# A hybrid two-layer decoder trunk: state-space pairs turned back by VectorE instead of GpSimd, gate channel computed in column groups, mixer order and start cut differently

## The reference, cut to what matters

```python
h = x + 0.5 * swiglu(rms(x))                 # 1024 -> 2 x 2816 -> 1024
u = rms(h);  proj = u @ w_in                 # one projection feeds four mixers
y_sb  = stick_breaking_attention(q, k, v)    # 4 heads of 64
y_s5  = s5_mixer(s5_u, ...)                  # 16 groups, 1024 complex states
y_gla = gla_mixer(gq, gk, gv, gr, gg, ...)   # z = gg @ w_gate, gg is 16 channels wide
y_dsa = dilated_mixer(q, k, v, ...)
per_branch = einsum('bsnw,nwd->bsnd', branches, w_branch)
mixed = sum(sigmoid(gates) * per_branch)     # gates: 4 x 1024 channels of proj
h = h + mixed @ w_out
h = h + 0.5 * swiglu(rms(h))
```

## Time and profile before

| | |
|---|---|
| median of three runs | 1290.23 us |
| profiled execution | 1289.22 us, span 1287.3 us |
| PE busy | 1245.8 us (97%) |
| DVE / ACT / POOL busy | 895.5 / 640.0 / 327.4 us |
| weight rounding: ACT L812, DVE L1072 | 407.2 us, 518.0 us |
| mixer of layer 0 | about 222 to 440 us of the span |
| mixer of layer 1 | about 858 to 1076 us |
| granted PE clock, mean | 0.992 |

### The profile page before, as it was taken

How to read it: one execution, slowest core, us unless ns; L and a number is a source line. 1 busy time by engine, 2 the same in 40 slices (tenths; PEclk the granted TensorE clock), 3 DMA queues, 4 the chain that set the end, 5 groups by cost and what they waited for, 6 DMA issues and landing times.

```text
span 1287.3 us, 25597 instructions
## 1 busy us (share of the span) xinstructions
PE 1245.8 (97%) x10328; PEld 1222.4 (95%) x10328; DVE 895.5 (70%) x1172; ACT 640.0 (50%) x904; POOL 327.4 (25%) x462
## 2 busy tenths in 40 slices
PE   5999999999999999999999999999999999999998
PEld 5999999888999999999999999998889999999998
DVE  4766857877877676555676687687887786656554
ACT  5654545663544454444456445557625444534432
POOL 0388800364003300000005895005630041000000
PEclk9999999998999999999999999999999999999999
DMA  7555554542344365555545545544333454555541
GB/s 299 199 185 174 180 179 165 175 149 99 131 158 166 135 236 198 191 195 168 191 135 201 188 165 200 189 164 152 135 130 131 154 186 160 201 184 175 186 173 66
DMA packets 31029, 220.46 MB, mean 171 GB/s; under 512 B 3568, under 2 KB 3568, under 8 KB 4592
## 3 DMA queue, kind: packets, MB, share of 16 engines
q1 hardware_dynamic: 30960, 219.49, 49.0%
HBM read 218.42 MB, written 1.05 MB: 170 GB/s over the span
## 4 chain that ended last, share of the span: by engine, by line
PE 75%; DVE 12%; POOL 7%; ACT 3%; issue 2%; DMA 0%; DVEq 0%; SPq 0%; ACTq 0%
PE banks L456 24%; PE banks L457 24%; PE banks L458 24%; DVE w_lo_t L1072 5%; PE banks L469 3%; ACT w_hi_t L812 1%; POOL st L1631 1%; DVE s5x L1274 1%; POOL s5x L1629 1%; POOL s5x L1628 1%; POOL st L1634 1%; POOL st L1536 1%; POOL st L1632 1%; DVE u_lo_t L1084 1%; DVE hT L1223 1%
## 5 line engine op out<-in xcount | busy, mean ns | idle before, releaser
L1072 DVE TENSOR_TENSOR w_lo_t<-raw,w_hi_t 128x1024 fp32r<-128x1024 f32 x408 | 518.0, 1310 | 107.8 <-ACT w_hi_t L812 107.4
L812 ACT ACTIVATE w_hi_t<-raw 128x1024 fp32r<-128x1024 f32 x408 | 407.2, 1046 | 126.7 <-PE banks L458 126.0
L456 PE MATMUL banks<-u_hi_t,w_hi_t 128*128 128x256 f32 x1520 | 436.0, 287 | 18.2 <-DVE w_lo_t L1072 14.1
L457 PE MATMUL banks<-u_lo_t,w_hi_t 128*128 128x256 f32 x1520 | 431.9, 284 | 0.0
L458 PE MATMUL banks<-u_hi_t,w_lo_t 128*128 128x256 f32 x1520 | 431.9, 284 | 0.0
L456 PEld LDWEIGHTS banks<-u_hi_t,w_hi_t 128*128 128x128 f32 x1520 | 293.6, 193 | 22.5 <-DVE w_lo_t L1072 14.1
L457 PEld LDWEIGHTS banks<-u_lo_t,w_hi_t 128*128 128x128 f32 x1520 | 293.8, 193 | 0.1
L458 PEld LDWEIGHTS banks<-u_hi_t,w_lo_t 128*128 128x128 f32 x1520 | 293.5, 193 | 0.0
L456 PE MATMUL banks<-b_hi_t,w_hi_t 128*128 128x256 f32 x864 | 245.1, 284 | 1.9 <-DVE b_lo_t L1084 1.9
L457 PE MATMUL banks<-b_lo_t,w_hi_t 128*128 128x256 f32 x864 | 244.5, 283 | 0.0
L458 PE MATMUL banks<-b_hi_t,w_lo_t 128*128 128x256 f32 x864 | 244.5, 283 | 0.0
(11 more groups left out here) (215 smaller groups left out, 1267.7 us busy)
## 6 DMA issues: line engine op xcount, KB each, us to landing
raw<-weights SPq DMA_DIRECT2D x203, 1024.0 KB, 4.9
prm<-params SPq DMA_DIRECT2D x1, 1178.5 KB, 5.3
prm<-params SPq DMA_DIRECT2D x1, 1166.5 KB, 15.1
cst<-constants SPq DMA_DIRECT2D x1, 1027.0 KB, 11.1
hT<-x_t SPq DMA_DIRECT2D x2, 512.0 KB, 5.5
raw<-weights SPq DMA_DIRECT2D x2, 512.0 KB, 6.4
out_t<-hT SPq DMA_DIRECT2D x4, 256.0 KB, 2.2
prm<-params SPq DMA_DIRECT2D x1, 12.0 KB, 1.9
```

The lines of the kernel that those rows point to most:

```text
L456: pe.matmul(o, st[0], mv[0], start=start, stop=False, skip_group_check=True)
L457: pe.matmul(o, st[0], mv[1], start=False, stop=False, skip_group_check=True)
L812: act.activation(w_hi[:, slot, a:a + HALF], raw[:, slot, a:a + HALF], ACT.Copy) \
L1072: dve.tensor_tensor(w_lo[:, slot, a:a + HALF], raw[:, slot, a:a + HALF], w_hi[:, slot, a:a + HALF].bitcast(F32), ALU.subtract).then_inc(s. ...
```

## The change

- `s5_pair` leaves POOL. DVE gets `s5_back`: two products of 128x1024 and two sums of 128x512 for each pair, and `s5_rotate`, `s5_scan`, `s5_back` of a pair now stand together in DVE's `pieces(m)`, m = 1, 4, 7, 10. PE's `s5_out` stands two blocks after `s5_in` instead of four.
- Block "gg" is gone. PE's `gate_channels` in `pieces(1)` computes the 16 channels from u_hi and u_lo with 16 fp32 matmuls (K 128, 32 output columns) that go round four column groups of the array; a `w_gate` with its rows repeated four times sums the groups.
- `SEQ` has 30 entries: without gg, with (0,1) before gv, and with (1,2), (1,3) before (0,2), (0,3). `OUT_TILES` has six: tiles 4 and 5 get a block each.
- DVE at index 22 and at `out3`, and ACT at `out3`, do their steps in another order; PE's `out0` waits for three of the four b_lo, and for the fourth just before it is used.
- At the start x and the first weight block come in quarters, and PE's first block waits for each quarter by itself. ACT gets one tiny activation before x lands.
- Constants shrink by 127 columns, parameters grow by 144.

```diff
-SEQ = ["s5u", "sbq", "sbk", "gg", "gqk", "dq", "dk", (0, 0), "sbv", "gv", (0, 1), "dv", "gr", (1, 0), (1, 1),
-       (0, 2), (0, 3), (1, 2), (1, 3), (2, 0), (2, 1), (2, 2), (2, 3),
+SEQ = ["s5u", "sbq", "sbk", "gqk", "dq", "dk", (0, 0), "sbv", (0, 1), "gv", "dv", "gr", (1, 0), (1, 1),
+       (1, 2), (1, 3), (0, 2), (0, 3), (2, 0), (2, 1), (2, 2), (2, 3),
        (3, 0), "out0", (3, 1), "out1", (3, 2), "out2", (3, 3), "out3"]
-OUT_TILES = [(0, 1), (2, 3), (4, 5), (6,), (7,)]
+OUT_TILES = [(0, 1), (2, 3), (4,), (5,), (6,), (7,)]
-MIXED_AT = [((0,), (1,)), ((), ()), ((), ()), ((2, 3, 4, 5, 6), (7,))]
+MIXED_AT = [((0,), (1,)), ((), ()), ((), ()), ((2, 3, 4, 5), (6, 7))]
...
# PE
+                    def gate_channels():
+                        for n, (part, half) in enumerate(itertools.product(range(2), range(2))):
+                            for j in range(4):
+                                kt = 4 * half + j
+                                a = PARAM["w_gg"][0] + 16 * kt
+                                ins = single(banks[32 * j:32 * j + 32, 2, T:2 * T], prm[:, a:a + 32],
+                                             u_hi[:, kt, :].bitcast(F32) if part == 0 else u_lo[:, kt, :].bitcast(F32),
+                                             n == 0, n == 3)
+                        ins.then_inc(s.gg, 1)
                     def pieces(m):
+                        if m == 1:
+                            gate_channels()
                         if m in S5_AT:
                             s5_in(S5_AT.index(m))
-                        if m - 4 in S5_AT:
-                            s5_out(S5_AT.index(m - 4))
+                        if m - 2 in S5_AT:
+                            s5_out(S5_AT.index(m - 2))
...
                         if q == 0:
-                            pe.wait_ge(s.b_lo, layer * PER.b_lo + 4)
+                            pe.wait_ge(s.b_lo, layer * PER.b_lo + 3)
...
                             for n in range(4):
+                                if (q, dt, n) == (0, 0, 3):
+                                    pe.wait_ge(s.b_lo, layer * PER.b_lo + 4)
...
# ACT, start
+            act.activation(nrm[:, 0, :], prm[:, 0:2], ACT.Copy)
+            act.wait_ge(s.w_used, 1)
+            for q in range(4):
+                split_pair(0, "g_ffn1", q)
+                act.wait_ge(s_first[q] if q < 3 else landed[0], 16)
+                a = QUARTER * q
+                act.activation(w_hi[:, 0, a:a + QUARTER], raw[:, 0, a:a + QUARTER], ACT.Copy) \
+                    .then_inc(s.q_hi if q % 2 == 0 else s.w_hi, 1)
...
# DVE
+                def s5_back(pair):
+                    dve.wait_ge(s.s5_scan, layer * PER.s5_scan + pair + 1)
+                    if pair >= 1:
+                        dve.wait_ge(s.s5_y, layer * PER.s5_y + pair)
+                    wide = lambda x: x[:, 2 * pair:2 * pair + 2, :].unsqueeze(2).to_broadcast([P, 2, 2, T])
+                    dve.tensor_tensor(st[:, :, :, :], s5x[:, :, 1, :, :], wide(rotS), ALU.mult)
+                    own.link(dve.tensor_tensor(s5x[:, :, 0, :, :], s5x[:, :, 1, :, :], wide(rotC), ALU.mult))
+                    dve.tensor_tensor(st[:, :, 1, :], s5x[:, :, 0, 0, :], st[:, :, 1, :], ALU.subtract)
+                    dve.tensor_tensor(st[:, :, 0, :], s5x[:, :, 0, 1, :], st[:, :, 0, :], ALU.add) \
+                        .then_inc(s.s5_state, 1)
...
                     if m in S5_AT:
                         s5_rotate(S5_AT.index(m))
-                    if m - 1 in S5_AT:
-                        s5_scan(S5_AT.index(m - 1))
+                        s5_scan(S5_AT.index(m))
+                        s5_back(S5_AT.index(m))
...
                         if is_branch(m):
                             q = int(SEQ[m][3])
+                            gate(2 * q)
                             if q == 3:
                                 for dt in range(2, 6):
                                     mixed_lo(dt)
-                            gate(2 * q)
+                                gate(2 * q + 1)
                             rest_of_weights(layer, k0 + m // RING + 1, m % RING)
-                            gate(2 * q + 1)
+                            if q < 3:
+                                gate(2 * q + 1)
                             continue
...
+                        if m == 22:
+                            pieces(m)
                         rest_of_weights(layer, k0 + m // RING + 1, m % RING)
...
# POOL
-                for pair in range(ST // 2):
-                    s5_pair(pair)
```

More of the change, by code:

```diff
@@ L389, in build @@
         s.pool = sem("pool")
-        s_x = [sem("x_landed0"), sem("x_landed1")]
+        s_x = [sem(f"x_landed{q}") for q in range(4)]
         s_gain = sem("gains_landed")
-        s_first = sem("first_half_landed")
+        s_first = [sem(f"first_quarter_landed{q}") for q in range(3)]
         s_const = sem("const_landed")
@@ L473, in block_ready, with in_part, in_block @@
                     pe.wait_ge(s.w_lo, layer * PER.w_lo + 2 * b + 8)
-                def in_part(b, slot, bank, where, kts, tiles=2):
+                def in_part(b, slot, bank, where, kts):
                     for kt in kts:
-                        for ct in range(tiles):
-                            last = kt == KT - 1 and ct == tiles - 1
+                        for ct in range(2):
+                            last = kt == KT - 1 and ct == 1
                             three(banks[:, bank, ct * T:(ct + 1) * T], w(slot, kt * 256 + ct * P, P),
                                   act_tiles(kt, where=where), kt == 0 and ct == 0, last, s.w_used if last else None)
-                def in_block(b, slot, bank, where=0, tiles=2):
+                def in_block(b, slot, bank, where=0):
                     block_ready(b)
-                    in_part(b, slot, bank, where, range(KT), tiles)
+                    in_part(b, slot, bank, where, range(KT))
                 def first_two(b, bank, norm, where):
                     for n, (j, q) in enumerate(STRAIGHT):
-                        if q == 0:
+                        if layer == 0 and norm == 0 and j == 0:
+                            if q % 2 == 0:
+                                pe.wait_ge(s.q_lo, q // 2 + 1)
+                            else:
+                                pe.wait_ge(s.w_lo, 2 * RING + (q + 1) // 2)
+                        elif q == 0:
                             block_ready(b + j)
@@ L600, in s5_out @@
                     def s5_out(pair):
-                        pe.wait_ge(s.s5_state, layer * PER.s5_state + 2 * pair + 2)
+                        pe.wait_ge(s.s5_state, layer * PER.s5_state + pair + 1)
                         if pair == 0:
@@ L794, in ffn_steps @@
             return (0 if f == 0 else FFN_BLOCKS + MIX_BLOCKS) // RING
-        def first_block(layer, k, slot):
-            return layer == 0 and isinstance(k, int) and k == 0 and slot == 0
         @block.scalar
@@ L1257, in s5_rotate @@
                     else:
-                        dve.wait_ge(s.s5_state, layer * PER.s5_state + 2 * pair)
+                        dve.wait_ge(s.s5_state, layer * PER.s5_state + pair)
                     i = 2 * pair
@@ L1706, in ffn @@
         s[at + FFN_BLOCKS - 4:at + FFN_BLOCKS] = a[-2], a[-1], o[-2], o[-1]
-    first = {"sbq": 0, "sbk": 256, "sbv": 512, "s5u": 768, "gqk": 1024, "gv": 1280, "gr": 1536, "gg": 1792,
+    first = {"sbq": 0, "sbk": 256, "sbv": 512, "s5u": 768, "gqk": 1024, "gv": 1280, "gr": 1536,
              "dq": 1808, "dk": 2064, "dv": 2320}
```

125 lines of the change are left out of this document (57 added, 68 removed).

## The result

The changed kernel takes **1309.76 us** (median of four runs, 1309.13 to 1313.4) against 1289.94 for the kernel before on the same chip: a ratio of 1.0167, 95% interval 1.0129 to 1.0205. It is slower by 1.7%. The forecast was 1306 us, slower the likeliest.

A forecast was written before the change was run, and what follows sets the result against it. PE, busy 97% of the span, was taken as the bound, so PE work, waits and clock count: 1289.2 profiled + 18.2 (9.1 a layer) - 2.4 (start) + 1.5 (clock) = 1306 us; range 1282 to 1315.

The forecast's parts named there:

- Chain on DVE: State-space work in DVE's queue, layer 0: pairs of 9.5 us in one piece, idle behind ACT, attention at 318.8.
- Attention's delay: Attention of layer 0 begins at 318.8 instead of 304.25, +14.5 us.
- 1.0, 2.0, 2.5, 7.1 and 2.8 us of PE waits: PE's waits before the attention: state 1, state 2, stick-breaking sums, state 3, masks.
- The clock: Half-clock loss after waits and through the attention: +1.5 us taken between ends of +3.7 and -3.7.
- Behind the attention: Rest of the layer: one full block fewer -5.8, turned dqk -0.5, `out0` +1.3, mixer's end -0.4.
- The 1.3 of `out0`: `out0` right behind block 22 waits for DVE's evacuation and b_lo of the gated branch, +1.3 us.
- Mixer's end: Wait of 1.9 us goes, two waits of 1.8 replace one of 0.95; with the later tail -0.4.
- the later tail: Named as part of the mixer's end sum of -0.4 us, without a size of its own.
- Start: Quarters let PE begin near 7.3 instead of 14.1, row broadcast near 22.6 or 23.1: -2.4 us, ends -3 and 0.
- Gate channel: Block gg's 2.9 us a layer go, fp32 matmuls in four column groups cost 2.0; the end does not move.
- DVE absorbs it: Rival 1: DVE takes the new work in its idle time, masks ready by 304, 1272 us; chance 0.13.
- a part of the overlap only: How far the trace shows POOL slowing DVE: 0.7 us a pair of halves, less than the skill's exclusion rule implies.

The follow-up runs named there:

- b2_ends: a4 with three swaps on DVE: gated branch's rest before an evacuation; at the mixer's end weights' rest before a split, last residual before last weights' rest; 1269.37 us.
- a3: The changed kernel with x and the first weights in halves, as in the kernel before; 1311.97 us, ratio 1.0181.
- b5: b3 with x and the first weights in halves, as in the kernel before; 1262.88 us, ratio 0.9779.
- a2: The changed kernel with its state-space part as before: POOL turns back, scans at m + 1, state outputs at m + 4; 1290.67 us, ratio 0.9999.
- a4: The changed kernel with rotate, scans and turning back on DVE in three successive pieces instead of one, state outputs at m + 4; 1283.62 us, ratio 0.9958.
- b3: a4 with the masks of heads 2 and 3 one index earlier on DVE and the swaps of b2_ends; 1263.45 us, ratio 0.9784.
- d1: b3 with POOL turning the pairs back, as in a2; 1271.77 us, ratio 0.9847.

## Why the prediction was right, and where it was off

- **Chain on DVE, right.** Forecast for layer 0: state 3 at 314.9, masks and attention at 318.8. Measured: 315.28, 319.17 and 319.27, with a start that came 1.7 us later than before, so the stage itself came out about 1 us shorter than forecast. The order of waits was right too. A pair takes 9.8 us, forecast 9.5. That DVE idles behind ACT at index 9 and 10 was right (3.19 and 3.49 us, forecast 3.3 and 3.5). At 7 it was 2.45, not 3.7: the term had ACT load its table after the evacuation.
- **Attention's delay.** Forecast +14.5 us; measured from the row broadcast of its mixer, 98.5 against 85.1 us, +13.4 in layer 0 and +13.5 in layer 1.
- **The waits came out smaller.** The terms had 1.0, 2.0, 2.5, 7.1 and 2.8 us of PE waits in a layer, 15.4; there were 11.3. Part of what is missing is time at half clock: PE arrived later at the wait for state 3, which DVE ended no later for it.
- **The clock is the term that was mis-sized.** +1.5 taken; in the mixers the loss rose by 9.3 us (19.5 against 10.2), and 3.2 came at the start. Not all of it reaches the end, since what PE loses ahead of a wait for DVE or POOL only shortens that wait. The kernel before shows it: it lost 1.7 us behind 884.03 and then waited 0.72 us for the next state, where layer 0 waited 2.36, and both layers reached the attention 85 us behind the row. In the changed kernel 2.6 and 2.5 us are of this kind. Behind the attention the loss rose by 2.1 us in layer 0 and 3.7 in layer 1: +5.8 for the +1.5. The prediction said "the waits are longer now" and still took the middle of its two ends, and it had no term for the start.
- **Behind the attention.** Forecast -5.4 a layer without clock (-5.8, -0.5, +1.3, -0.4); from the attention to the next row broadcast measured -3.3 and -0.8, and with the clock's 2.1 and 3.7 us taken out -5.4 and -4.5. The 1.3 of `out0` measured 1.43.
- **Mixer's end, waits right, clock not seen.** Forecast -0.4 a layer, in which the prediction's own waits make +0.7 (-1.9, +3.6, -0.95) and the other -1.1 is "the later tail", without a working; no run shows it, and the wait at the tail was 1.11 us where 1.01 stood before. From the end of `out3` to the row broadcast it was 38.5 us instead of 37.9, +0.6. The wait of 1.90 for the last gate product went, as said. The one-tile blocks had 1.91 and 0.34 where 1.8 twice was forecast and 0.95 stood before, so the waits did shrink. The 1.6 us at a clock of 0.57 behind the first of them outweigh that. And b2_ends shows that neither was a price of one-tile blocks, only of two DVE steps' order.
- **Start, wrong.** Forecast -2.4, measured +1.7 in the profile and zero in time (a3, b5). PE's first matmul was right (7.03, forecast 7.3). Two steps failed. First, ACT got the next two blocks later: its waits for transfers end at 14.10 and 18.91, where the prediction took the 17.38 of before for the second. So the sum of squares, put near 18, came at 20.44 (DVE's part at 18.32, before 16.85), and the root was ready at 24.3, a little before the 24.6 of the kernel before:

```profile
24.15 0.16 DVE L1161 TENSOR_TENSOR rstd<-nrm 128x2 f32<-128x2 f32 x1
```

  Second, PE reached the row broadcast only 2.9 us after that, at 27.20, because its matmuls behind the wait of 5.16 us ran at half clock. The forecast of the start has no term for that.
- **Gate channel, right.** 32 instructions in 1.86 us (224.31 to 226.17), forecast 2.0. By the estimate from the Trainium skill ("TensorE: Matmul & The Clock Gate", "Why this matters for your kernels"), 3.4 us for three column tiles' worth of overlap, it would have been nearly twice that; the four groups here overlap more than the three of which the Trainium skill speaks. As forecast, it didn't matter: a2 has it and is at 0.9999.
- **The rivals.** "DVE absorbs it" failed at the point that it named, masks by 304. But its reasons were sound: a4 and b3 absorb all of the new work, and d1 shows POOL's silence is worth something. Since a4 with one more reordering ran at 1275.0 and 1269.4, what kept the change from the rival's 1272 us was DVE's order. But the same reorderings with POOL turning back (d1) give 1271.8 too, so only 8 us of the way down come from the move itself. The Trainium skill's rule that a GpSimd instruction and a DVE instruction with two SBUF inputs exclude each other ("SBUF — State Buffer", "SBUF: two separate sides") agrees with this case's trace. POOL's products in the kernel before:

```profile
258.72 2.77 POOL L1628 TENSOR_TENSOR s5x<-s5x,G 128x256 f32<-128x256 f32 x1 [10.35 <-DVE s5x L1274]
...
307.27 1.70 POOL L1629 TENSOR_TENSOR s5x<-s5x,G 128x256 f32<-128x256 f32 x1
308.94 1.70 POOL L1631 TENSOR_TENSOR st<-s5x,G 128x256 f32<-128x256 f32 x1
310.60 0.72 POOL L1632 TENSOR_TENSOR st<-s5x,G 128x256 f32<-128x256 f32 x1
```

  A product takes 0.72 us where no weight half runs, 1.70 beside one half and 2.77 where it came behind a pair that began first (258.56, 2.33 us, not slowed). The two halves that took 3.05 us are the 2.35 of a pair alone and one product between them. The prediction read this as "a part of the overlap only"; it is whole instructions in turn. Over the run DVE's halves took 11.6 us less without POOL's pairs.

By stage the misses are +4.1 at the start, -1.1 and -1.0 up to the attention, +4.3 of clock behind it, and 0.0 and +0.9 for the rest behind it: 7.2 us, about the distance to the profiled execution (the terms add up to 1306.5). They partly cancel, and the median lies 3.6 us below the profiled execution, so that the forecast is within 4 us of it is in part luck. The start's sign was wrong and the clock's rise was about four times the term; the delay of the attention, on which the forecast rests, was right to 8%.

## What to carry to other kernels

On an in-order queue ask of a new piece not how much it is but how long it is in one go, and what stands behind it: here the same 14 us of work a layer cost 20 us in one piece and saved 6 in three. When a wait is named, move the waiter first in thought: if what stands next on the releaser's queue is wanted right after, the wait only changes its name. And give the clock behind a TensorE wait a line of its own in the sum: here waits of 1.9 to 5.2 us cost up to 5.7 us more in matmuls at half clock. Of that loss, count only what lies behind the last wait that another engine ends: what comes ahead of it only shortens the wait.
